# Experts' gate and up products with the weights still and 128 tokens streaming

## The chip, the cores and the metric

One Trainium2 chip, one of its cores. The metric is device time in microseconds (us) of one execution; the lower the better. The whole program is one launch.

## The reference, cut to what matters

The program runs two transformer blocks of two layers each over 256 tokens of width 1024, in float32. The change touches one part of it, the mixture of experts that closes the first block:

```
def swiglu(h, w_gate, w_up, w_down):
    return (jax.nn.silu(h @ w_gate) * (h @ w_up)) @ w_down

def moe_swiglu(h, w_router, w_gate, w_up, w_down):
    ...
    for e in range(N_EXPERTS):                       # 8 experts, top 2 of 8 are chosen for each token
        out = out + gates[..., e:e + 1] * swiglu(h, w_gate[e], w_up[e], w_down[e])
```

Here `h` is tokens x 1024, `w_gate[e]` and `w_up[e]` are 1024 x 2816, `w_down[e]` is 2816 x 1024.

## The kernel before, in words

Every weight is cut into units of 128 x 1024 numbers (512 KB). SyncE issues their loads into a ring of R = 11 slots (`raw`). ScalarE copies each unit to `whi` rounded to float32r (`split_high`, L436; a ring of H = 6 slots), and VectorE forms the remainder `low` (`split_low`, L440). A product of nearly full precision is then three float32r matmuls into the same PSUM: high x high (L445), high x low (L446), low x high (L447), by `product`. The activations are kept in the same two parts: `hTh` and `hTl` (hidden transposed), `aTh` and `aTl` (expert activation transposed).

The experts are one function, `swiglu`, on each engine, called inside a hardware loop over the 8 experts. Each expert gathers its (at most 128) tokens by a matmul with a one-hot matrix (`gather`, L1193), which also transposes them into `hTh`/`hTl`. It then takes STEPS = 11 steps of FW = 256 of the 2816 hidden columns. Step j has four "gu" units and two "down" units. A gu unit holds two 128-row slices of the input dimension, each with 256 gate and 256 up columns. Three things follow one another on TensorE in step j:

- the gate and up products of step j: for each of 8 slices of the input dimension, the tokens' slice (128 x 128) is the still operand and 512 weight columns stream (L1052); the result lies in one PSUM bank, tokens on partitions, with gate in columns 0 to 255 and up in 256 to 511;
- the transposes of the activation of step j - 1 (L1068), from `act` in SBUF into PSUM bank 6;
- the down products of step j - 2, with `aTh`/`aTl` still and 512 columns of `w_down` streaming.

ScalarE takes silu of the gate half (`gu_silu`, L1388) and VectorE multiplies it by the up half into `act` (L1858). After the transposes ScalarE copies bank 6 to `aTh` (L1392) and VectorE forms `aTl` (L1863). The next expert's gather and this expert's scatter of the previous result are woven between these through hooks. The order of the units is written out by `ffn_order`: down lags gu by two steps. Two PSUM banks, 4 and 5, take turns for gate and up (`gu_bank`).

The dense feed-forward stages elsewhere in the program (`dense`) already use the other form: a block of 128 weight columns is still and 256 tokens stream.

Of the kernel before, what the change touches and what calls it, by code (L numbers as in the profile page):

```python
# [24 lines left out]
P = 128  # L25
# [177 lines left out]
def build(nc, g, out, ctx):  # L203
# [171 lines left out]
    def high_slot(f, n):  # L375

        return (n + (N_MOE if f is fb else 0)) % H
# [65 lines left out]
    def product(pe, dst, ah, al, bh, bl, start, stop, **kw):  # L443

        pe.matmul(dst, ah, bh, start=start, stop=False, **kw)  # L445
        pe.matmul(dst, ah, bl, start=False, stop=False, **kw)  # L446
        return pe.matmul(dst, al, bh, start=False, stop=stop, **kw)  # L447
# [70 lines left out]
    def gu_bank(j, tiles):  # L518

        if tiles == T:  # L520
            return 0 if j == 0 else 4
        return 4 + j % 2
# [219 lines left out]
    def _(pe):  # L742
# [291 lines left out]
        def swiglu(f, n0, step0, tiles, it=0, first=(), hooks=None, gate=None):  # L1034

            units, steps = FFN_UNITS * it, STEPS * it
            for j in range(STEPS + 2):
                if j < STEPS:
                    if j == 0:
                        for sm, v in first:  # L1040
                            pe.wait_ge(sm, v)
                    elif j > 1 or tiles == 1:
                        pe.wait_ge(f.act, step0 + j + steps - (1 if tiles == 1 else 0))
                    for u in range(4):
                        n = n0 + POS["gu", j, u]
                        pe.wait_ge(f.lo, n + 1 + units)
                        for t in range(tiles):
                            for kk in range(2):
                                if j == 0 and t == 0 and hooks is None:
                                    pe.wait_ge(s_htl, first_ht + 2 * u + kk + 1)  # L1050
                                k = 2 * u + kk
                                last = product(pe, ps[:, gu_bank(j, tiles) + t, :],  # L1052
                                               hTh[:, k, t * P:(t + 1) * P], hTl[:, k, t * P:(t + 1) * P],
                                               whi[:, high_slot(f, n), kk * 512:(kk + 1) * 512],
                                               low[:, raw_slot(f, n), kk * 512:(kk + 1) * 512],
                                               start=k == 0, stop=k == DC - 1)
                        last.then_inc(f.used, 1)
                if hooks is not None and ("before_T", j) in hooks:
                    hooks["before_T", j]()
                if 1 <= j <= STEPS:  # L1060
                    i = j - 1
                    pe.wait_ge(f.act, step0 + i + 1 + steps)
                    if not (isinstance(it, int) and step0 + i == 0):
                        pe.wait_ge(f.atl, step0 + i + steps)
                    for t in range(tiles):
                        for kk in range(FK):
                            at = kk * S + t * P
                            last = pe.transpose(ps[:, 6, at:at + P], act[:, t, kk * P:(kk + 1) * P], ident)  # L1068
                    last.then_inc(f.tr, 1)
                if hooks is not None and ("after_T", j) in hooks:  # L1070
                    hooks["after_T", j]()
                if j == STEPS and gate is not None:
                    sum_gate(gate)
                if j >= 2:
                    i = j - 2

                    def unit(kk, t, half):
                        n = n0 + POS["down", i, kk]
                        return product(pe, ps[:, 2 * t + half, :],
                                       aTh[:, i % 2, kk, t * P:(t + 1) * P],  # L1080
                                       aTl[:, i % 2, kk, t * P:(t + 1) * P],
                                       whi[:, high_slot(f, n), half * 512:(half + 1) * 512],
                                       low[:, raw_slot(f, n), half * 512:(half + 1) * 512],
                                       start=i == 0 and kk == 0, stop=i == STEPS - 1 and kk == FK - 1)

                    pe.wait_ge(f.atl, step0 + i + 1 + steps)
                    for kk in range(FK):
                        pe.wait_ge(f.lo, n0 + POS["down", i, kk] + 1 + units)
                        if i < STEPS - 1 or tiles == 1:
                            for t in range(tiles):  # L1090
                                for half in range(2):
                                    last = unit(kk, t, half)
                            last.then_inc(f.used, 1)
                    if i == STEPS - 1 and tiles == T:
                        for t in range(T):
                            for half in range(2):
                                if (t, half) != (T - 1, 1):
                                    unit(0, t, half)
                                    unit(1, t, half).then_inc(s_part, 1)
                                else:  # L1100
                                    unit(0, t, half).then_inc(f.used, 1)
                                    unit(1, t, half).then_inc(f.used, 1)
            if gate in (1, 5):
                sum_cols(gate + 1)
# [182 lines left out]
    def _(ac):  # L1287
# [87 lines left out]
        def swiglu(f, n0, step0, tiles, it=0, skip=0, hooks=None, opening=None):  # L1375
            k = skip
            for j in range(STEPS + 2):
                while k < split_ahead(j):
                    if k == H and opening is not None:
                        opening()  # L1380
                    split_high(ac, f, n0 + k, it)
                    k += 1
                if j < STEPS:
                    ac.wait_ge(f.used, n0 + POS["gu", j, 3] + 1 + FFN_UNITS * it)
                    if not (isinstance(it, int) and step0 + j == 0):
                        ac.wait_ge(f.act, step0 + j + STEPS * it)
                    b = gu_bank(j, tiles)
                    ac.activation(gu_silu[:, 0:tiles, :], ps[:, b:b + tiles, 0:FW], ACT.Silu).then_inc(f.silu, 1)  # L1388
                if 1 <= j <= STEPS:
                    i = j - 1  # L1390
                    ac.wait_ge(f.tr, i + 1 + STEPS * it)
                    ac.activation(aTh[:, i % 2, :, 0:tiles * P],  # L1392
                                  ps[:, 6, :].rearrange("p (k s) -> p k s", k=FK)[:, :, 0:tiles * P], ACT.Copy)\
                        .then_inc(f.ath, 1)
                if hooks is not None and j in hooks:
                    hooks[j]()
# [265 lines left out]
    def _(ve):  # L1662
# [180 lines left out]
        def swiglu(f, n0, step0, tiles, it=0, skip=0, hooks=None, between=0, opening=None):  # L1843
            k = 0
            for j in range(STEPS + 2):
                while k < split_ahead(j):
                    if k == H and opening is not None:
                        opening()
                    if k >= skip:
                        split_low(ve, f, n0 + k, it)  # L1850
                    mods(spread(between, MOD_FFN_OVER, k - MOD_FFN_FROM))
                    k += 1
                if j < STEPS:
                    ve.wait_ge(f.silu, step0 + j + 1 + STEPS * it)
                    if not (isinstance(it, int) and j == 0):
                        ve.wait_ge(f.tr, j + STEPS * it)
                    b = gu_bank(j, tiles)
                    ve.tensor_tensor(act[:, 0:tiles, :], gu_silu[:, 0:tiles, :], ps[:, b:b + tiles, FW:2 * FW],  # L1858
                                     ALU.mult).then_inc(f.act, 1)
                if 1 <= j <= STEPS:  # L1860
                    i = j - 1
                    ve.wait_ge(f.ath, step0 + i + 1 + STEPS * it)
                    ve.tensor_tensor(aTl[:, i % 2, :, 0:tiles * P],  # L1863
                                     ps[:, 6, :].rearrange("p (k s) -> p k s", k=FK)[:, :, 0:tiles * P],
                                     aTh[:, i % 2, :, 0:tiles * P].bitcast(F32), ALU.subtract).then_inc(f.atl, 1)
                if hooks is not None and j in hooks:
                    hooks[j]()
# [554 lines left out]
```

## Time and profile before

| what | value |
|---|---|
| median of 2 runs | 1983.2 us (1980.59 and 1985.81) |
| span of the profiled execution | 1978.7 us |
| TensorE matmul busy | 1862.4 us, 94% of the span, 10670 instructions |
| TensorE weight load busy | 1603.6 us, 81% |
| VectorE busy | 1638.0 us, 83% |
| ScalarE busy | 1141.5 us, 58% |
| HBM read | 548.38 MB, 278 GB/s over the span |

The span runs from the first to the last instruction of the profiled execution; the page gives no other time for that execution, so the 4.5 us between the span and the median stand for what lies outside it. "Busy" on TensorE overlaps between neighbouring matmuls, since they are pipelined and their ends are modelled; how far apart two starts lie says more than how long one row is. TensorE's weight loads are rows of their own ("PEld") and run beside the matmul before. The experts take the stretch from about 500 to 1290 us.

### The profile page before, as it was taken

What the parts mean: (1) busy time and instruction counts of PE and PEld (TensorE: products, weight loads), DVE (VectorE), ACT (ScalarE), POOL (GpSimd) and SP (SyncE); (2) the same over time, 40 slices, a digit from 0 to 9 for tenths busy, and PEclk for the clock granted to TensorE, in tenths of its full rate; (3) what the DMA queues carried; (4) which work ended last, traced back from release to release, by engine and by line L of the source; (5) the groups of instructions that cost most, each with busy time, mean ns of one, the idle gap of its engine ahead of it and who ended that gap; (6) DMA issues with size and microseconds to landing.
All of it is one profiled execution on the core that took longest, in us unless ns stands there. A gap on an engine that the chain in (4) does not pass through costs nothing.

```text
span 1978.7 us, 32211 instructions
## 1 busy us (share of the span) xinstructions
PE 1862.4 (94%) x10670; PEld 1603.6 (81%) x10670; DVE 1638.0 (83%) x2193; ACT 1141.5 (58%) x1616; POOL 36.1 (2%) x47
## 2 busy tenths in 40 slices
PE   3999998988999999999999999988799998889998
PEld 2989998866788888888888888866689997679997
DVE  7999995768999999999999989887887758887554
ACT  3445444454777777777777777754654435545443
POOL 2000000000000000000000000000000000000000
PEclk9999999999999999999999999988999999999999
DMA  9978995557799999999999999958478874845772
GB/s 326 352 250 308 384 365 154 172 177 244 261 343 359 344 361 341 359 341 360 341 361 341 360 341 359 339 191 244 142 234 279 283 262 148 245 159 189 224 222 80
DMA packets 368485, 551.26 MB, mean 279 GB/s; under 512 B 35827, under 2 KB 293110, under 8 KB 368342
## 3 DMA queue, kind: packets, MB, share of 16 engines
q1 hardware_dynamic: 365392, 547.81, 82.3%
q10 hardware_dynamic: 2118, 1.46, 0.3%
q8 instruction: 65, 1.06, 0.2%
q14 instruction: 78, 0.64, 0.1%
q0 software_dynamic: 832, 0.30, 0.1%
HBM read 548.38 MB, written 1.08 MB: 278 GB/s over the span
## 4 chain that ended last, share of the span: by engine, by line
PE 84%; DVE 9%; ACT 3%; issue 2%; DMA 1%; POOL 0%; DVEq 0%; ACTq 0%; POOLq 0%
PE ps L445 25%; PE ps L447 25%; PE ps L446 25%; ACT prob L1410 2%; PE ps L960 2%; PE ps L1193 2%; DVE units_low L440 1%; DVE mod_acc L1733 1%; PE ps L1068 1%; PE ps L945 1%; DVE x_tokens L1760 1%; PE ps L796 1%; DVE x_normed L1759 1%; PE ps L771 1%; PE ps L933 1%
## 5 line engine op out<-in xcount | busy, mean ns | idle before, releaser
L440 DVE TENSOR_TENSOR units_low<-raw_units,units_high 128x1024 fp32r<-128x1024 f32 (+1 forms) x838 | 982.7, 1218 | 144.9 <-ACT units_high L436 142.1
L436 ACT ACTIVATE units_high<-raw_units 128x1024 fp32r<-128x1024 f32 (+1 forms) x838 | 846.3, 1057 | 300.0 <-PE ps L447 267.8
L445 PE MATMUL ps<-units_high,hT_high 128*128 128x512 f32 (+1 forms) x1040 | 412.1, 396 | 1.6 <-DVE hT_low L2161 1.4
L447 PE MATMUL ps<-units_high,hT_low 128*128 128x512 f32 (+1 forms) x1040 | 408.8, 393 | 0.0
L446 PE MATMUL ps<-units_low,hT_high 128*128 128x512 f32 (+1 forms) x1040 | 405.9, 390 | 0.0
L445 PE MATMUL ps<-hT_high,units_high 128*128 128x256 f32 x1248 | 346.3, 277 | 6.5 <-DVE hT_low L1802 5.2
L446 PE MATMUL ps<-hT_low,units_high 128*128 128x256 f32 x1248 | 345.5, 277 | 0.0
L447 PE MATMUL ps<-hT_high,units_low 128*128 128x256 f32 x1248 | 345.5, 277 | 0.0
L445 PE MATMUL ps<-units_high,aT_high 128*128 128x512 f32 x632 | 255.1, 404 | 1.2 <-DVE qkT L1997 0.6
L447 PE MATMUL ps<-units_high,aT_low 128*128 128x512 f32 x632 | 248.7, 393 | 0.0
L446 PE MATMUL ps<-units_low,aT_high 128*128 128x512 f32 x632 | 247.1, 391 | 0.0
L445 PEld LDWEIGHTS ps<-hT_high,units_high 128*128 128x128 f32 x1248 | 235.0, 188 | 8.7 <-issue 6.0
L446 PEld LDWEIGHTS ps<-hT_low,units_high 128*128 128x128 f32 x1248 | 235.2, 188 | 1.1
L447 PEld LDWEIGHTS ps<-hT_high,units_low 128*128 128x128 f32 x1248 | 235.0, 188 | 0.0
L445 PEld LDWEIGHTS ps<-units_high,hT_high 128*128 128x128 f32 x1040 | 197.0, 189 | 46.2 <-issue 3.3
L447 PEld LDWEIGHTS ps<-units_high,hT_low 128*128 128x128 f32 x1040 | 196.4, 189 | 43.1
L446 PEld LDWEIGHTS ps<-units_low,hT_high 128*128 128x128 f32 x1040 | 196.8, 189 | 42.3 <-issue 0.2
L1733 DVE SCALAR_TENSOR_TENSOR mod_acc<-mod_in,silu_c,mod_acc 128x1024 f32<-128x1024 f32 x168 | 213.9, 1280 | 9.5 <-DMA mod_in<-in_mod_w 3.7
L447 PEld LDWEIGHTS ps<-units_high,aT_low 128*128 128x128 f32 x632 | 118.7, 188 | 25.7
L445 PEld LDWEIGHTS ps<-units_high,aT_high 128*128 128x128 f32 x632 | 118.9, 188 | 24.4 <-issue 1.7
L446 PEld LDWEIGHTS ps<-units_low,aT_high 128*128 128x128 f32 x632 | 119.0, 188 | 23.7 <-issue 1.0
L1388 ACT ACTIVATE gu_silu<-ps 128x256 f32<-128x256 f32 x88 | 33.8, 384 | 145.0 <-PE ps L447 145.0
(283 smaller groups left out, 1430.2 us busy)
## 6 DMA issues: line engine op xcount, KB each, us to landing
raw_units<-in_moe_w_gate SPq DMA_DIRECT2D x352, 256.0 KB, 4.5
raw_units<-in_moe_w_up SPq DMA_DIRECT2D x352, 256.0 KB, 5.8
raw_units<-in_moe_w_down SPq DMA_DIRECT2D x176, 512.0 KB, 6.3
mod_in<-in_mod_w SPq DMA_DIRECT2D x96, 512.0 KB, 6.8
mod_in<-in_w_mod SPq DMA_DIRECT2D x96, 512.0 KB, 5.4
raw_units<-in_w_gu SPq DMA_DIRECT2D x176, 256.0 KB, 3.8
raw_units<-in_w_down SPq DMA_DIRECT2D x44, 512.0 KB, 4.2
raw_units<-in_w_in SPq DMA_DIRECT2D x32, 512.0 KB, 6.8
```

The lines of the kernel that those rows point to most:

```text
L436: eng.activation(whi[:rows, high_slot(f, n), 0:width], raw[:rows, raw_slot(f, n), 0:width], ACT.Copy).then_inc(f.hi, 1)
L440: eng.tensor_tensor(low[:rows, raw_slot(f, n), 0:width], raw[:rows, raw_slot(f, n), 0:width], whi[:rows, high_slot(f, n), 0:width].bitcast ...
L445: pe.matmul(dst, ah, bh, start=start, stop=False, **kw)
L446: pe.matmul(dst, ah, bl, start=False, stop=False, **kw)
L447: return pe.matmul(dst, al, bh, start=False, stop=stop, **kw)
L771: last = pe.matmul(ps[:, bank + half, :], ones, gate_acc(m)[:, half * 512:(half + 1) * 512], start=True, stop=True)
L796: last = pe.transpose(ps[:, 4 + b, at:at + P], xn[:, t, c * P:(c + 1) * P], ident)
L960: last = pe.matmul(dst, probT[:, j % 2, qt * key_tiles(second, 0) + kt, :], qkv[:, at - left * HD:at + (1 + right) * HD], start=kt == 0, s ...
L1193: last = pe.matmul(ps[:, 2 + c // 4, (c % 4) * P:(c % 4 + 1) * P], xn[:, t, c * P:(c + 1) * P], hot[:, t, :], start=t == 0, stop=t == T - 1)
L1388: ac.activation(gu_silu[:, 0:tiles, :], ps[:, b:b + tiles, 0:FW], ACT.Silu).then_inc(f.silu, 1)
L1410: last = ac.activation(prob[:, i % 2, qt, 0:nk], prob[:, i % 2, qt, 0:nk], ACT.Exp, bias=negm(qt, h), scale=-1.0, accum_out=sums(qt, h))
L1733: ve.scalar_tensor_tensor(out=acc, in0=mod_in[:, q % MOD_SLOTS, :], scalar=silu_c[:, at:at + 1], in1=acc, op0=ALU.mult, op1=ALU.add).then_ ...
```

## The change

In `swiglu`, gate and up are formed transposed. For each slice of the input dimension, four blocks of 128 weight columns (gate 0, gate 1, up 0, up 1) become the still operand one after the other and the 128 tokens of `hTh`/`hTl` stream. The result has hidden columns on partitions and tokens along the free dimension, four groups of 128 columns in the same PSUM bank, gate groups in the first half and up groups in the second. So `act` comes out transposed already: TensorE's transposes, their wait and their semaphore go, ScalarE copies `act` to `aTh` and VectorE subtracts from `act` instead of from PSUM, and `act` gets two buffers by turns. VectorE's write of `act` waits for the readers of two steps before (`f.ath`, `f.atl`) in place of `f.tr`; ScalarE's copy waits for `f.act` and for the last down unit that read the same half of `aTh`.

```
-                        for t in range(tiles):
-                            for kk in range(2):
...
-                                last = product(pe, ps[:, gu_bank(j, tiles) + t, :],
-                                               hTh[:, k, t * P:(t + 1) * P], hTl[:, k, t * P:(t + 1) * P],
-                                               whi[:, high_slot(f, n), kk * 512:(kk + 1) * 512],
-                                               low[:, raw_slot(f, n), kk * 512:(kk + 1) * 512],
-                                               start=k == 0, stop=k == DC - 1)
+                        for kk in range(2):
+                            k = 2 * u + kk
+                            for c in range(4):
+                                col = kk * 512 + c * P
+                                last = product(pe, ps[:, gu_bank(j, tiles), c * P:(c + 1) * P],
+                                               whi[:, high_slot(f, n), col:col + P],
+                                               low[:, raw_slot(f, n), col:col + P],
+                                               hTh[:, k, 0:P], hTl[:, k, 0:P], start=k == 0 and c == 0,
+                                               stop=k == DC - 1, skip_group_check=True)
...
-                if 1 <= j <= STEPS:
-                    i = j - 1
-                    pe.wait_ge(f.act, step0 + i + 1 + steps)
-                    if not (isinstance(it, int) and step0 + i == 0):
-                        pe.wait_ge(f.atl, step0 + i + steps)
-                    for t in range(tiles):
-                        for kk in range(FK):
-                            at = kk * S + t * P
-                            last = pe.transpose(ps[:, 6, at:at + P], act[:, t, kk * P:(kk + 1) * P], ident)
-                    last.then_inc(f.tr, 1)
...
-                    ac.wait_ge(f.tr, i + 1 + STEPS * it)
-                    ac.activation(aTh[:, i % 2, :, 0:tiles * P],
-                                  ps[:, 6, :].rearrange("p (k s) -> p k s", k=FK)[:, :, 0:tiles * P], ACT.Copy)\
+                    ac.wait_ge(f.act, step0 + i + 1 + STEPS * it)
+                    ac.wait_ge(f.used, n0 + FFN_UNITS * it + (POS["down", i - 2, FK - 1] + 1 if i >= 2 else 0))
+                    ac.activation(aTh[:, i % 2, :, 0:P], act[:, i % 2, :].rearrange("p (k s) -> p k s", k=FK), ACT.Copy)\
...
-                        ve.wait_ge(f.tr, j + STEPS * it)
+                        ve.wait_ge(f.ath, step0 + max(j - 1, 0) + STEPS * it)
+                        ve.wait_ge(f.atl, step0 + max(j - 1, 0) + STEPS * it)
...
-                    ve.tensor_tensor(act[:, 0:tiles, :], gu_silu[:, 0:tiles, :], ps[:, b:b + tiles, FW:2 * FW],
-                                     ALU.mult).then_inc(f.act, 1)
+                    ve.tensor_tensor(act[:, j % 2, :], gu_silu[:, 0, :], ps[:, b, FW:2 * FW], ALU.mult).then_inc(f.act, 1)
...
-                    ve.tensor_tensor(aTl[:, i % 2, :, 0:tiles * P],
-                                     ps[:, 6, :].rearrange("p (k s) -> p k s", k=FK)[:, :, 0:tiles * P],
+                    ve.tensor_tensor(aTl[:, i % 2, :, 0:P],
+                                     act[:, i % 2, :].rearrange("p (k s) -> p k s", k=FK),
                                      aTh[:, i % 2, :, 0:tiles * P].bitcast(F32), ALU.subtract).then_inc(f.atl, 1)
```

## Rows read from the trace of the kernel before

**Rows 1.** The page: busy time of each engine, and the span in 40 slices

```profile
PE 1862.4 (94%) x10670; PEld 1603.6 (81%) x10670; DVE 1638.0 (83%) x2193; ACT 1141.5 (58%) x1616; POOL 36.1 (2%) x47
...
PE   3999998988999999999999999988799998889998
...
PEclk9999999999999999999999999988999999999999
DMA  9978995557799999999999999958478874845772
```

**Rows 2.** Busy time by stretch: the middle of the experts' stage, and one expert

```profile
core 0: us, PE busy (x) PEld busy (x) DVE busy (x) ACT busy (x) POOL busy (x), PEclk, DMA share, GB/s
600.00:1200.00 600.00, 600.00 (x2791) 495.15 (x2790) 541.66 (x583) 446.05 (x553) 0.00 (x0) 1.00 1.03 351
592.70:691.59 98.89, 98.89 (x463) 81.62 (x462) 89.16 (x97) 73.57 (x91) 0.00 (x0) 1.00 1.03 351
```

**Rows 3.** Waits between 600 and 1200 us, all engines: in total, times, longest

```profile
ACT gu_silu L1388 <- PE ps L447: 109.6, 66, 1.8
ACT aT_high L1392 <- PE ps L1068: 24.8, 6, 4.1
...
DVE units_low L440 <- ACT units_high L436: 15.8, 42, 0.4
```

**Rows 4.** Groups between 500 and 1300 us: what the experts run on TensorE

```profile
L445 PE MATMUL ps<-units_high,hT_high 128*128 128x512 f32 x704 | 276.4, 393 | 1.4 <-DVE hT_low L2161 1.4
...
L445 PE MATMUL ps<-units_high,aT_high 128*128 128x512 f32 x352 | 144.4, 410 | 0.0
...
L1068 PE MATMUL ps<-table,act 128*128 128x128 f32 x176 | 33.5, 272 | 0.0
```

**Rows 5.** Order of time, TensorE, 512-column products: first and last of 48

```profile
799.62 0.39 PE L445 MATMUL ps<-units_high,hT_high 128*128 128x512 f32 x1
...
810.37 0.40 PE L447 MATMUL ps<-units_high,hT_low 128*128 128x512 f32 x1
```

**Rows 6.** Order of time, TensorE, around one step's transposes

```profile
589.33 0.40 PE L447 MATMUL ps<-units_high,hT_low 128*128 128x512 f32 x1
589.56 0.38 PE L1068 MATMUL ps<-table,act 128*128 128x128 f32 x2
589.70 0.48 PE L445 MATMUL ps<-units_high,aT_high 128*128 128x512 f32 x1
590.01 0.39 PE L446 MATMUL ps<-units_low,aT_high 128*128 128x512 f32 x1
```

**Rows 7.** The chain that ended last, around one gather and its successor

```profile
592.70 3.57 PE ps L1193 x32
...
691.59 3.57 PE ps L1193 x32
```

**Rows 8.** Order of time, TensorE, a dense stage: first and last of 34

```profile
282.05 0.28 PE L447 MATMUL ps<-hT_high,units_low 128*128 128x256 f32 x1
...
285.79 0.28 PE L447 MATMUL ps<-hT_high,units_low 128*128 128x256 f32 x1
```

**Rows 9.** Order of time, TensorE, products that stream 8 columns

```profile
495.31 0.39 PE L1182 MATMUL ps<-router_tmp,table 128*128 128x8 f32 x2 [0.20 <-DVE router_tmp L2138]
495.55 0.37 PE L1183 MATMUL ps<-router_tmp,table 128*128 128x8 f32 x2
...
496.22 0.37 PE L1186 MATMUL ps<-router_tmp,table 128*128 128x8 f32 x2
496.44 0.71 PE L778 MATMUL ps<-hT_high 128*128 128x512 f32 x2
```

**Rows 10.** Groups of weight loads: 128 columns, and 16 columns

```profile
L446 PEld LDWEIGHTS ps<-hT_low,units_high 128*128 128x128 f32 x1248 | 235.2, 188 | 1.1
...
L1157 PEld LDWEIGHTS ps<-hT_low,router_high_low 128*16 128x16 f32 x8 | 0.8, 95 | 0.1
```

**Rows 11.** Busy time in a stretch of attention

```profile
424.00:436.00 12.00, 9.12 (x73) 6.78 (x73) 11.46 (x28) 10.42 (x33) 0.00 (x0) 1.00 0.60 173
```

**Rows 12.** Order of time, TensorE, 512-column products where the clock was low

```profile
455.79 0.63 PE L446 MATMUL ps<-units_low,hT_high 128*128 128x512 f32 x1
456.22 0.63 PE L447 MATMUL ps<-units_high,hT_low 128*128 128x512 f32 x1
```

More of the change, by code:

```diff
@@ L1046, in swiglu @@
                         pe.wait_ge(f.lo, n + 1 + units)
-                        for t in range(tiles):
-                            for kk in range(2):
-                                if j == 0 and t == 0 and hooks is None:
-                                    pe.wait_ge(s_htl, first_ht + 2 * u + kk + 1)
-                                k = 2 * u + kk
-                                last = product(pe, ps[:, gu_bank(j, tiles) + t, :],
-                                               hTh[:, k, t * P:(t + 1) * P], hTl[:, k, t * P:(t + 1) * P],
-                                               whi[:, high_slot(f, n), kk * 512:(kk + 1) * 512],
-                                               low[:, raw_slot(f, n), kk * 512:(kk + 1) * 512],
-                                               start=k == 0, stop=k == DC - 1)
+                        for kk in range(2):
[7 more added lines that the diff above has]
+                                               stop=k == DC - 1, skip_group_check=True)
                         last.then_inc(f.used, 1)
```

## The prediction

> **What bounds the kernel now.** I began with the page's busy shares and its 40 slices [rows 1]. The reader is to see that TensorE is at 9 in every slice of the experts' stage (slices 11 to 25 or so), that DMA is at 9 there too, and that the granted clock is full. Two resources look full, so the next question is which one waits for the other. The table by stretch [rows 2] has TensorE busy for 600.00 of 600 us in the middle of the experts, VectorE for 541.66, ScalarE for 446.05. One expert takes 98.89 us, which is also the distance between two gathers in the chain that ended last [rows 7]. The waits settle it: between 600 and 1200 us every long wait is of an engine that waits for TensorE, or for another that does [rows 3]; none is of TensorE for anything, and nobody waits long for a DMA. So TensorE's own rate of products sets the end. The 351 GB/s is what that rate draws, not a limit that is felt: the loads run ahead through 11 slots and wait for `f.used`.
>
> So the change is a question of how many matmuls there are and how far apart they start. I take distances between starts, not the length of a row: rows of neighbouring matmuls overlap.
>
> **What is removed.** Gate and up of one step are 4 units x 2 slices x 3 products = 24 matmuls of 512 columns; of one expert 264 (the page's count, 704 for 8 experts in each of three forms, gives the same: 2112 / 8) [rows 4]. Forty-eight starts of this kind span 10.75 us, 47 distances: 0.2287 us each [rows 5]. That is 264 x 0.2287 = 60.4 us in each expert. The transposes start at 589.56; without them the first down product would start there and the second at 589.79; it starts at 590.01 [rows 6]. So a pair costs TensorE 0.22 us, 11 pairs 2.4 us in an expert. Together 62.8 us of the 98.9 us go. The check on the method: 396 products of 512 columns x 0.2287 = 90.6, the gather 3.57 [rows 7], 8 scatter products of the same width 1.8, transposes 2.4 + 0.2 for the pair on the one-hot matrix: 98.6 against 98.9 measured.
>
> **What is added.** The same columns of weights now need a still load each: 4 blocks x 8 slices x 3 products = 96 matmuls with 128 columns streaming in a step, 1056 in an expert. Each has a weight load of 128 columns. Before, one load served 512 streamed columns; now it serves 128. The question is the distance p between starts.
>
> - By the stream alone: 256 columns go by at 0.1133 us (3.74 us over 33 distances) [rows 8], 512 at 0.2287, so the stream costs 0.45 ns for a column and 128 columns would take 0.057 us.
> - By the load: products that stream only 8 columns, and so have almost no stream, still start 0.113 us apart (10 records from 495.31 to 496.44) [rows 9]. Nothing but the load of 128 columns is left to set this. The lengths of the loads say the same: 188 ns for 128 columns, 95 for 16 [rows 10]; 93 ns over 112 columns are 0.83 ns for a column, and 128 of them 106 ns, which is occupied once in each product, however well the constant part overlaps.
> - Load and stream together: the gather has 128-column loads and 128-column streams in the same stage, beside the same traffic: 32 records in 3.57 us, 0.1116 us each [rows 7]. As its operands are plain float32, each record may stream more slowly than float32r does; even so load and stream overlap wholly.
>
> So p is the greater of load and stream, not their sum. The lowest value I allow is 0.106 (the load without any constant), the highest 0.113 to 0.115 (8-column products, and some for the start of each unit). I take 0.112, next to the gather, the nearest row in shape and place. Then 1056 x 0.112 = 118.3 us in each expert.
>
> **Weighed against this.** The rows show no 128-column load at under 0.11 us a product. The Trainium skill, page TensorE: Matmul & The Clock Gate, section Back-to-back issue gap, gives about 81 ns for a product of 128 columns in a sustained stream of loads and matmuls. By that figure an estimate would be 1056 x 0.081 = 85.5 us, 22.7 us more in an expert and about 2165 us in all. The same page, Weight-path perf modes, excludes FP32 weights from its faster load, which suggests that the 81 ns are for narrower types; no run here shows those.
>
> **Edits I cost at nothing.** ScalarE's `aTh` copy and VectorE's `aTl` have the same 256 elements from SBUF in place of PSUM; both engines had 25 and 10 us idle in an expert [rows 2] and get more. If a read from SBUF costs more, the 55 us that are added to TensorE cover it. The new wait of VectorE for `f.ath`/`f.atl` of two steps before: behind it are `split_low`s of the next units, which TensorE needs; but the ScalarE copy it waits for stands behind no more than the silu of a step earlier, and lies a whole step, now about 14 us, back. ScalarE's new wait for `f.used` names the down unit of two steps before, which TensorE ended before it began the gate and up whose silu ScalarE has just done. TensorE's wait before the transposes goes; down products still wait for `f.atl`, which now comes earlier. None of these was late before [rows 3] and TensorE gets slower, so nothing else becomes late. TensorE issues two instructions (load and matmul) each 0.112 us, as the dense stage does at 0.1133 without stalls [rows 8], so instruction supply isn't new. SyncE's loads keep their order and only get later; with some 154 us for the same bytes DMA drops to about two thirds of its rate.
>
> **The sum.** In an expert +118.3 - 60.4 - 2.4 = +55.5 us; eight experts +444 us. On the span 1978.7 + 444 = 2423; the median lies 4.5 us above the span, so 2427 us. All of it is on the path, since TensorE has no gap in the stage to absorb any. With p = 0.106 it is +49.1 x 8 = +393, 2376 us; with 0.115 it is +58.6 x 8 = +469, 2452 us.
>
> **The rivals.**
>
> - Narrow float32r streams are slow. No row has a float32r matmul with under 256 columns. The nearest row on the dear side is the gather: a plain float32 product of 128 columns is two records, 0.223 us. If a narrow float32r product cost that, or the 0.2287 of the 512-column one, an expert would need 236 to 241 us for gate and up: +173 to +179, in all 3366 to 3412 us. For it: the kernel has no such width anywhere, so nothing excludes it. Against: 512, 480 and 256 columns show no step, 0.1133 is half of 0.2287. Chance 0.11, at about 3390.
> - Loads aren't hidden behind so short a stream: p = 0.106 + 0.057 = 0.163, +109.3 x 8 = +874, 2857 us. The gather speaks against it. Chance 0.03.
> - The other side: the load is no floor for these tiles, for instance because loads of float32r blocks overlap one another more than those of the float32 products that I read. Then the stream decides, p = 0.057, 60.2 us in place of 62.8: 2.6 us less in an expert, 1962 us, not slower than before. The place is gate and up alone, the price is 1056 x p, and the change breaks even at p = 62.8 / 1056 = 0.0595 us. For it: in the dense stage a load of 188 ns starts every 113 ns, so loads do overlap in part. Against it: the 8-column products, where a shorter distance had every chance to show. The page's 81 ns would lie between, on the slower side. Chance for p well under 0.106: 0.04.
> - The clock falls. TensorE would stream half as densely in two thirds of the stage. At the lower level of 1.2 GHz 512 columns start 0.43 us apart in place of 0.2287 [rows 12]; if the whole stage went so, 154.4 us for an expert become 309, and the program takes 3660 us. Against: attention, with 73 products and 9.12 us of 12 busy, kept the full 2.4 GHz [rows 11]. Chance 0.02.
>
> That the change doesn't do what it says isn't open: each product names a 128-column block, and the loads are counted above.
>
> **How the numbers follow.** The forecast, load-bound products at 0.106 to 0.115 us, has 0.80; the others 0.11, 0.03, 0.04 and 0.02. The predicted time is the forecast's, 2427 us. Its own bounds are 2376 and 2452; I go from 2385, as 0.106 leaves out a constant that every row shows, to 2465, for some loss at the 352 starts of units. That holds nearly all of the 0.80 and leaves the other cases out. Two per cent is about what a measurement of this kernel can tell from no change. Only the case with the stream as bound ends inside it, and a still better one beyond it: faster 0.01, same 0.03, slower 0.96.
>
> **What would show it.** Right: in the experts a group of 128x128 float32r products, 2816 in each of three forms, starting 0.112 us apart; L1068 gone; an expert at some 154 us; weight loads nearly as many microseconds as the stretch has; TensorE without waits and a granted clock of 1.00; DMA share at about 0.66; VectorE and ScalarE idle for longer, both behind TensorE. Wrong: a distance of 0.22 (slow narrow streams) or 0.163 (loads in series), a granted clock under 0.95, or a wait of TensorE for `aT_low` or `units_low` in the steps. The sum stands on p more than on all the rest: 0.001 us of it is 8.4 us of the program.

## The result, and the profile after

The changed kernel takes 2434.83 us (median of 2419.12 and 2450.54) against 1983.2 us before: 1.227 times as long, interval 1.222 to 1.231. The forecast was 2427 us. Four more executions, on another occasion, gave 2422.94 to 2443.99.

The page of the profiled execution (2450.54 us, span 2448.3 us), the lines that answer to [rows 1]:

```profile
PE 2331.8 (95%) x16830; PEld 2160.9 (88%) x16830; DVE 1655.7 (68%) x2193; ACT 1153.3 (47%) x1616; POOL 36.1 (1%) x47
...
PE   5999999899999999999999999999987999988998
...
PEclk9999999968999999999999999999999999999999
DMA  8969955726777767677677776777756788584673
```

The reader is to see four things: TensorE stays at 9 and has 6160 records more (8448 narrow products in, 2112 wide ones and 176 transposes out); DMA, at 9 in the experts before, is down to 6 and 7; VectorE and ScalarE did the same work in a longer time (VectorE's share falls from 83% to 68%); and the granted clock shows a 6 and an 8 in slices 9 and 10, where there was none before.

Busy time by stretch, answering to [rows 2], and the waits between 600 and 1600 us, answering to [rows 3]:

```profile
core 0: us, PE busy (x) PEld busy (x) DVE busy (x) ACT busy (x) POOL busy (x), PEclk, DMA share, GB/s
520.00:560.00 40.00, 40.00 (x186) 39.61 (x185) 11.99 (x12) 9.08 (x11) 0.00 (x0) 0.50 0.33 104
700.00:1300.00 600.00, 599.97 (x4797) 576.72 (x4797) 353.67 (x374) 290.52 (x355) 0.00 (x0) 1.00 0.72 226
```

```profile
ACT gu_silu L1377 <- PE ps L447: 310.9, 71, 4.7
DVE act L1848 <- ACT gu_silu L1377: 252.1, 71, 3.8
ACT units_high L436 <- PE ps L447: 180.3, 144, 1.6
```

In the second row of the first view TensorE and its weight loads are both busy nearly all the time; before, the loads were at 495 of 600. The rate fell from 351 to 226 GB/s, which is 0.64 of it, as forecast; the DMA share itself is 0.72, where 0.66 was expected. The first row is the odd one, and the one sign of being wrong that did appear in part (a granted clock under 0.95): TensorE is just as busy, at a granted clock of 0.50, which is 1.2 GHz. The waits say who sets the pace: everybody still waits for TensorE.

Order of time on TensorE, first and last of 28 gate and up products, answering to [rows 5]; and the same in the stretch of low clock, first and last of 12:

```profile
799.77 0.28 PE L447 MATMUL ps<-hT_high,units_low 128*128 128x128 f32 x1
...
802.79 0.27 PE L447 MATMUL ps<-hT_high,units_low 128*128 128x128 f32 x1
```

```profile
519.62 0.41 PE L446 MATMUL ps<-hT_low,units_high 128*128 128x128 f32 x1
...
521.97 0.41 PE L445 MATMUL ps<-hT_high,units_high 128*128 128x128 f32 x1
```

The distance between starts is 3.02 / 27 = 0.1119 us at full clock, and 2.35 / 11 = 0.2136 us at the low one. The chain that ended last, answering to [rows 7], gives one expert:

```profile
678.96 3.57 PE ps L1182 x32
...
832.84 3.57 PE ps L1182 x32
```

153.88 us for an expert, 98.89 before. It adds up: 1056 x 3.02 / 27 = 118.1, 132 down products x 0.2287 = 30.2, gather 3.57, scatter 1.8, the one-hot transposes 0.2: 153.9 us. TensorE has no gap here.

The low stretch begins in the first expert, 2.2 us after its first product, and lasts from 506.81 to 568.15 us, so 61.3 us:

```profile
504.63 0.33 PE L445 MATMUL ps<-hT_high,units_high 128*128 128x128 f32 x1 [1.41 <-DVE hT_low L2150]
...
506.70 0.32 PE L445 MATMUL ps<-hT_high,units_high 128*128 128x128 f32 x1
506.81 0.42 PE L446 MATMUL ps<-hT_low,units_high 128*128 128x128 f32 x1
...
543.73 0.73 PE L1195 MATMUL ps<-y_high,scatter_hot 128*128 128x512 f32 x1
...
565.91 0.73 PE L1195 MATMUL ps<-y_high,scatter_hot 128*128 128x512 f32 x1
...
568.15 0.43 PE L446 MATMUL ps<-units_low,aT_high 128*128 128x512 f32 x1
568.42 0.40 PE L447 MATMUL ps<-units_high,aT_low 128*128 128x512 f32 x1
```

Ahead of it TensorE had been idle for 1.41 us. Four scatter products of 512 columns at 543.73 did not bring the clock back; four more and the first down product, from 565.91 on, did.

### The profile page after: what moved, and what is told of

Read it like the earlier page. It is cut to its first block, busy times and chain, and to the rows that moved or that the text cites. A ratio compares the mean times of both kernels' runs of the same rounds, so it can differ in the third digit from the quotient of the medians.

```text
span 2448.3 us, 44475 instructions
## 1 busy us (share of the span) xinstructions
PE 2331.8 (95%) x16830; PEld 2160.9 (88%) x16830; DVE 1655.7 (68%) x2193; ACT 1153.3 (47%) x1616; POOL 36.1 (1%) x47
## 4 chain that ended last, share of the span: by engine, by line
PE 87%; DVE 7%; ACT 3%; issue 2%; DMA 1%; DVEq 0%; SPq 0%; ACTq 0%
PE ps L445 27%; PE ps L447 27%; PE ps L446 27%; PE ps L1182 1%; ACT prob L1399 1%; PE ps L960 1%; DVE units_low L440 1%; DVE mod_acc L1722 1%; PE ps L945 1%; DVE x_tokens L1749 1%; PE ps L796 1%; DVE x_normed L1748 1%; DMA mod_in<-in_w_mod 0%; PE ps L771 0%; PE ps L1195 0%
## 5 line engine op out<-in xcount | busy, mean ns | idle before, releaser
L445 PE MATMUL ps<-hT_high,units_high 128*128 128x128 f32 (+1 forms) x4064 | 1128.2, 278 | 8.2 <-DVE hT_low L1791 5.2
L446 PE MATMUL ps<-hT_low,units_high 128*128 128x128 f32 (+1 forms) x4064 | 1131.2, 278 | 0.0
L447 PE MATMUL ps<-hT_high,units_low 128*128 128x128 f32 (+1 forms) x4064 | 1131.1, 278 | 0.0
L445 PEld LDWEIGHTS ps<-hT_high,units_high 128*128 128x128 f32 x4064 | 787.8, 194 | 15.9 <-issue 7.8
L446 PEld LDWEIGHTS ps<-hT_low,units_high 128*128 128x128 f32 x4064 | 787.4, 194 | 4.4
L447 PEld LDWEIGHTS ps<-hT_high,units_low 128*128 128x128 f32 x4064 | 787.7, 194 | 0.0
L445 PE MATMUL ps<-units_high,hT_high 128*128 128x512 f32 (+1 forms) x336 | 135.9, 404 | 0.5 <-DVE hT_low L1791 0.4
L447 PE MATMUL ps<-units_high,hT_low 128*128 128x512 f32 (+1 forms) x336 | 132.6, 395 | 0.0
L446 PE MATMUL ps<-units_low,hT_high 128*128 128x512 f32 (+1 forms) x336 | 132.5, 394 | 0.0
L445 PEld LDWEIGHTS ps<-units_high,hT_high 128*128 128x128 f32 x336 | 64.9, 193 | 18.6 <-issue 3.5
```

## The experiments

Unless its section says otherwise, a kernel starts from the changed one. Edits are shown in `swiglu` on TensorE where nothing else is said.

### narrow_again: the changed kernel once more

> The changed kernel once more. Every theory of the distance between products (load, stream, issue) expects the time it had, about 2420 to 2450 us, and 0.112 us between starts of gate and up products. On the clock: if the low stretch of 61 us at the start of the first expert is a chance event that not each execution has, the times spread, between about 2415 us (no such stretch) and 2450 us (a full one); if it belongs to the kernel, each run shows a mean granted clock of 0.976 and about 2450 us.

Measured: 2422.94, 2424.28, 2437.28 and 2443.99 us, with mean granted clocks of 0.985, 0.985, 0.980 and 0.978. The profiled one (2424.28, span 2422.1 us) has no low stretch in the experts at all, though TensorE was idle for the same 1.41 us ahead of its first expert; its seven later experts take 154.05 us on average. The other three have no trace. An estimate of how long each spent at 0.50, span x (1 - clock) / 0.5, gives 73 us for the two quick ones, as for the kernel before (71), and 97 and 107 for the others (117 for the execution with the low stretch of 61 us). So a low stretch in the experts belongs to some executions and not to others; that it was there in the two slower ones, and shorter, is inferred from their mean clock. Not all of the spread need be its doing: the kernel before, measured beside them, went from 1980.39 to 1993.81. Without the low stretch the changed kernel takes some 2424 us.

### half_stream: half the tokens stream behind the same loads

```
-  last = product(pe, ps[:, gu_bank(j, tiles), c * P:(c + 1) * P], ..., hTh[:, k, 0:P], hTl[:, k, 0:P], ...)
+  last = product(pe, ps[:, gu_bank(j, tiles), c * P:c * P + 64], ..., hTh[:, k, 0:64], hTl[:, k, 0:64], ...)
```

> Gate and up of the experts stream 64 tokens in place of 128 (the products for the other 64 tokens are left out); the loads stay. Load theory (a load of 128 columns sets the distance): still 0.11 us between starts, the time as of the changed kernel within 10 us, about 2425. Stream theory (narrow float32r streams cost 0.87 ns for a column, which is also 0.112 us for 128): the distance falls towards 0.06, 8448 products x 0.05 = 420 us less, about 2000. Issue theory (TensorE's sequencer needs 0.056 us for each of the two instructions): unchanged, about 2425.

Measured: 3126.76 us (3124.51 and 3129.0), some 700 us above what any theory said. The trace shows why, and answers the question nevertheless. Order of time on TensorE, at the start of the second expert, one of the places where the clock fell; the first two rows are the first and last of 27 at full clock, the other two the first and last of 16 at the low one:

```profile
747.58 0.28 PE L447 MATMUL ps<-hT_high,units_low 128*128 128x64 f32 x1
...
750.49 0.28 PE L446 MATMUL ps<-hT_low,units_high 128*128 128x64 f32 x1
...
750.98 0.40 PE L446 MATMUL ps<-hT_low,units_high 128*128 128x64 f32 x1
...
754.18 0.40 PE L446 MATMUL ps<-hT_low,units_high 128*128 128x64 f32 x1
```

At full clock 64 columns take 2.91 / 26 = 0.1119 us, exactly what 128 take. Load theory (or issue theory) holds, stream theory falls. Then the clock falls in the middle of an uninterrupted row of products, and the distance is 3.20 / 15 = 0.213 us. Busy time by stretch, before and after the fall, and over the stage:

```profile
742.00:748.00 6.00, 6.00 (x31) 5.00 (x30) 4.81 (x5) 5.87 (x7) 0.00 (x0) 1.00 0.53 160
...
754.00:760.00 6.00, 6.00 (x30) 6.00 (x30) 1.22 (x1) 1.06 (x1) 0.00 (x0) 0.50 0.28 95
...
700.00:2400.00 1700.00, 1699.88 (x8662) 1625.34 (x8662) 648.28 (x674) 537.31 (x639) 0.00 (x0) 0.62 0.48 144
```

TensorE is busy throughout and is granted 0.62 on average. Ahead of this fall it had run 512-column down products at full clock without a gap; with half the stream behind each load the products did not keep it.

### half_load: half the load, the same stream

```
-  ps[:, gu_bank(j, tiles), c * P:(c + 1) * P], whi[..., col:col + P], low[..., col:col + P], ...
+  ps[0:64, gu_bank(j, tiles), c * P:(c + 1) * P], whi[..., col:col + 64], low[..., col:col + 64], ...
```

> Gate and up of the experts have 64 weight columns still in place of 128 (the products for the other 64 of each block are left out); the 128 tokens stream as before. Load theory: the load falls to about half, the distance to that of the stream or a little over, 0.057 to 0.065 us, so 8448 x 0.05 = 400 to 465 us less: 1960 to 2030. Stream theory: unchanged, 0.112 us, about 2425. Issue theory: unchanged, about 2425.

Measured: 2018.42 us (2015.82 and 2021.01), some 406 us under the changed kernel without its low stretch. First and last of 48 products on TensorE:

```profile
819.83 0.23 PE L445 MATMUL ps<-hT_high,units_high 128*64 128x128 f32 x1
...
822.65 0.22 PE L447 MATMUL ps<-hT_high,units_low 128*64 128x128 f32 x1
```

2.82 / 47 = 0.0600 us. The same count of instructions starts at nearly half the distance, so neither the issue nor the stream of 128 columns set 0.112 us; the load of 128 weight columns did. The whole gains 406 us and not the full 8448 x 0.052 = 439. TensorE now waits for units, which is 15 us of the missing 33; the rest was not followed up. Waits between 600 and 1300 us:

```profile
PE ps L445 <- DVE units_low L440: 15.1, 6, 2.9
...
ACT units_high L436 <- DMA raw_units<-in_moe_w_up: 9.2, 20, 1.6
```

Behind such a wait the clock fell here too, but it came back without one wide product:

```profile
706.12 0.27 PE L445 MATMUL ps<-hT_high,units_high 128*64 128x128 f32 x1 [1.92 <-DVE units_low L440]
...
706.73 0.31 PE L447 MATMUL ps<-hT_high,units_low 128*64 128x128 f32 x1
...
709.71 0.31 PE L445 MATMUL ps<-hT_high,units_high 128*64 128x128 f32 x1
...
710.07 0.22 PE L446 MATMUL ps<-hT_low,units_high 128*64 128x128 f32 x1
```

The second and third rows are the first and last of 29 products at the low level, 2.98 / 28 = 0.106 us apart. From about 706.5 to 709.9 us, so 3.4 us, the clock is low, then the distance is 0.060 again. The changed kernel streams the same 128 columns at each product, but behind twice the load, and stayed low for 61 us.

### double_stream: 256 columns behind the same loads

```
-  ps[:, gu_bank(j, tiles), c * P:(c + 1) * P], ..., hTh[:, k, 0:P], hTl[:, k, 0:P], ...
+  ps[:, gu_bank(j, tiles), (c % 2) * S:(c % 2 + 1) * S], ..., hTh[:, k, 0:S], hTl[:, k, 0:S], ...
```

> Gate and up of the experts stream 256 columns in place of 128 behind the same loads (the other 128 columns are old activations, and the four blocks share two halves of the bank, so the sums aren't gate and up). Load theory: the stream now just fills the load's time, 0.1133 us as in the dense stages, 8448 x 0.0015 = 12 us more, about 2437. Stream theory (0.87 ns for a column, or a slow mode under 256 columns that ends here): 0.22 us, +900 us, or 0.1133. Issue theory: as load theory.

Measured: 2444.46 us (2444.24 and 2444.69). First and last of 31 products:

```profile
821.56 0.28 PE L447 MATMUL ps<-hT_high,units_low 128*128 128x256 f32 x1
...
824.97 0.28 PE L447 MATMUL ps<-hT_high,units_low 128*128 128x256 f32 x1
```

3.41 / 30 = 0.1137 us, in place of 0.1119. Twice the stream costs 20 us in all, where 12 were expected; 8448 x 0.0018 = 15 of them lie in the distance, the rest was not followed up. The profiled execution has no low stretch in the experts, and both runs agree within half a microsecond.

### old_no_transposes: one part of the change alone

The kernel before, with the change's lines for `act`, `aTh` and `aTl` on ScalarE and VectorE, and on TensorE:

```
-                if 1 <= j <= STEPS:
-                    i = j - 1
-                    pe.wait_ge(f.act, step0 + i + 1 + steps)
...
-                            last = pe.transpose(ps[:, 6, at:at + P], act[:, t, kk * P:(kk + 1) * P], ident)
-                    last.then_inc(f.tr, 1)
```

> The kernel before with one part of the change alone: gate and up keep the tokens still and 512 weight columns streaming, but the transposes and their wait are left out, and act goes straight from SBUF to aTh and aTl (so the down products get untransposed activations). If TensorE's own work is the bound, 88 x 0.22 us = 19 us go, about 1963, ratio 0.990. If the transposes' time would be filled by another wait (for a unit's low part, or a DMA at 351 GB/s), nothing goes: 1982.

Measured: ratio 0.9938, interval 0.9915 to 0.9961, so about 12 us gained (8 to 17), between the two expectations. The trace tells how each was right for a part of the experts. The chain that ended last, gathers of the first experts, and the waits between 600 and 1200 us:

```profile
591.05 3.57 PE ps L1183 x32
687.50 3.57 PE ps L1183 x32
783.98 3.57 PE ps L1183 x32
881.53 3.57 PE ps L1183 x32
```

```profile
ACT units_high L436 <- DMA raw_units<-in_moe_w_up: 61.2, 149, 1.2
DVE units_low L440 <- ACT units_high L436: 33.4, 110, 0.9
ACT units_high L436 <- DMA raw_units<-in_moe_w_down: 29.3, 83, 0.9
...
PEld ps L445 <- DVE units_low L440: 6.2, 20, 0.6
```

The first two experts take 96.45 and 96.48 us, 2.4 less than 98.89: that is the transposes' price as predicted. The next takes 97.55 and the later ones some 97.3. ScalarE now waits for DMA 232 times, which it hardly did before: 66 units of 0.524 MB in 97.3 us are 356 GB/s. Once the lead of the 11 slots is spent, the loads set the pace, and 1.6 of the 2.4 us stay. So the 351 GB/s of the kernel before was not its limit, but stood within 2% of one.

### gap_narrow, gap_old_form, gap_narrow_wide: can the narrow products lift the clock?

In gap_narrow (the changed kernel) and gap_old_form (the kernel before) ScalarE keeps TensorE waiting ahead of the first expert:

```
         for half in range(2):
+            if half == 1:
+                for _ in range(6):
+                    link(ac.activation(yh[:, :], xn[:, 0, :], ACT.Copy))
             ac.wait_ge(s_gat, half + 1)
```

gap_narrow_wide is gap_narrow with, on TensorE, after the first waits of expert 0:

```
+                            pe.wait_ge(f.lo, n0 + 1)
+                            slot = high_slot(f, n0)
+                            for _ in range(24):
+                                pe.matmul(ps[:, 6, :], whi[:, slot, 0:P], whi[:, slot, 0:512], start=True, stop=True)
```

> The changed kernel with an idle time of TensorE put in just before the first expert's gate and up: ScalarE makes six idle copies of 128x1024, each 1.0 us, ahead of the second half of the gathered tokens (6 us or so by themselves). Trap theory (with only 128 columns streamed behind each load of 128, TensorE is too little used to be given back its full clock once it has lost it; only the 512-column scatter and down products, which first come after two steps, do that): each execution now has the low stretch of 40 to 65 us, mean clock about 0.976, 2424 + 6 + 24 = 2454 or some more, with little spread. Chance theory (the long low stretch comes and goes whatever the work is): the spread of the changed kernel stays, 2430 to 2450, with no link to the gap.

> The kernel before with the same idle time. Trap theory: here 512 columns stream behind each load, so the clock may fall in the gap but is back within a few us of work: 1982 + 6 + 2 to 4 = 1990 to 1993. Chance theory or a long recovery whatever the work: 1982 + 6 + 20 to 30 = 2010 to 2018, with a low stretch of some 60 us.

> The changed kernel with the idle time, and then 24 idle products that stream 512 columns before the first narrow one (5.5 us at full clock, some 9 if they begin at the low one). Trap theory: they bring the clock back, and the narrow products keep it: no low stretch beyond a few us, 2424 + 6 + 5 to 9 = 2435 to 2440, less than with the gap alone although there is more work. Chance theory: as the gap alone plus 5 to 9, about 2460.

Measured: gap_narrow 2454.14 us (2446.86 to 2461.93), with a mean clock of 0.972 to 0.976 in all four executions. gap_old_form 1995.1 us, ratio 1.0036 (1.0016 to 1.0056): 3 to 11 us more than the kernel before, whose median was 1987.05 on this occasion. gap_narrow_wide 2438.68 us (2432.54 to 2446.84), clock 0.983 to 0.986: it does 24 products more than gap_narrow and is 15 us faster. Busy time by stretch of 20 us, gap_narrow first, then gap_old_form, then gap_narrow_wide; the last three numbers of a row are granted clock, DMA share and GB/s:

```profile
500.00:520.00 20.00, 13.17 (x77) 12.98 (x75) 11.58 (x21) 12.04 (x13) 0.00 (x0) 0.64 0.09 27
520.00:540.00 20.00, 20.00 (x95) 20.00 (x95) 5.23 (x5) 4.39 (x5) 0.00 (x0) 0.50 0.32 105
540.00:560.00 20.00, 20.00 (x120) 19.61 (x120) 6.98 (x8) 5.84 (x7) 0.00 (x0) 0.66 0.34 107
```

```profile
500.00:520.00 20.00, 12.78 (x66) 10.69 (x66) 12.74 (x29) 15.91 (x19) 0.00 (x0) 0.83 0.11 35
520.00:540.00 20.00, 20.00 (x91) 16.37 (x90) 20.00 (x22) 14.69 (x19) 0.00 (x0) 1.00 0.97 322
```

```profile
500.00:520.00 20.00, 13.17 (x82) 11.65 (x80) 9.90 (x20) 11.09 (x13) 0.00 (x0) 0.83 0.00 1
520.00:540.00 20.00, 20.00 (x178) 19.83 (x176) 9.24 (x10) 7.81 (x11) 0.00 (x0) 1.00 0.65 194
```

After the same idle time, 512-column products are back at full clock by 520 us. The narrow ones run at 0.50, busy without a break, through the next 20 us and into the third stretch; the clock is back at 553.4 us, right behind the first four scatter products (551.11 to 552.9). Wide products ahead of the narrow ones bring the clock back, and the narrow ones then keep it. Chance theory falls. All three times fit the trap theory, gap_old_form by its 8 us over the kernel before where the theory gave 8 to 11 (its 1995.1 itself is 2 us above the expected 1993). One thing does not fit it as worded: in the changed kernel's own trace the same four scatter products, at 543.73, did not bring the clock back. So some wide products are not always enough, and how many it takes was not measured; 24 were.

### bridged, wide_start: the changed kernel without the trap

bridged puts six such 512-column products ahead of the first wait, where TensorE idles 1.4 us after the first gather; wide_start puts 24 behind that wait. Neither has the gap of the three kernels above.

```
+                        if isinstance(it, int) and hooks is not None:
+                            pe.wait_ge(f.lo, n0 + 1)
+                            slot = high_slot(f, n0)
+                            for _ in range(6):
+                                pe.matmul(ps[:, 6, :], whi[:, slot, 0:P], whi[:, slot, 0:512], start=True, stop=True)
                         for sm, v in first:
                             pe.wait_ge(sm, v)
```

> The changed kernel with six idle products that stream 512 columns behind the first gather, while TensorE waits 1.4 us for the first expert's tokens, so at no cost of their own. Trap theory: TensorE comes to the narrow products without an idle time before them, and the clock is lost less often: mean granted clock 0.983 to 0.986 in all executions, 2420 to 2428, with no run at 2435 to 2450 as the changed kernel alone has them. If the narrow products lose the clock by themselves at the start of an expert, the spread of the changed kernel stays.

> The changed kernel with 24 idle products of 512 columns between the first wait and the first narrow product (5.5 us). Trap theory: no low stretch in the first expert in any execution, 2424 + 5.5 = 2430, mean clock 0.983 to 0.986, highest run under 2440. Otherwise the changed kernel's spread, 2428 to 2455.

Measured: bridged 2423.91 us (six executions, 2420.14 to 2430.66; clocks 0.984 to 0.987), at its highest 3 us above the expected 2428. wide_start 2432.47 us (five, 2426.17 to 2433.08; clocks 0.983 to 0.987). Neither profiled execution has a low stretch in the experts. Of the changed kernel's six executions three were at 2437 or above, with clocks of 0.980 or less; of these eleven none was. If it were chance, such a split would come once in 34 times (20 / 680). It is not a clean comparison either: the changed kernel did not run beside these two, and the kernel before spread less on this occasion (1979.96 to 1988.98). So that the wide products removed the low stretch is likely here, and not shown. bridged has the lowest median of all forms of the change, and is still 1.2215 times the kernel before (1.2190 to 1.2241), an interval that overlaps that of the changed kernel.

## Why the prediction was right

**The bound.** TensorE had no gap before and has none now; the added time of an expert is the added time of its products. The waits of both kernels confirm it, and so does an expert that adds up to 153.9 us from TensorE's records alone.

**The distance p.** Predicted 0.112, measured 0.1119 us. The reason given, that the load of 128 weight columns sets it and load and stream overlap wholly, was put to the test by changing each by itself: stream 64, 128 and 256 columns and p is 0.1119, 0.1119 and 0.1137; load 64 columns and it is 0.0600, where the stream alone would give 0.057. So p is the greater of the two, to within 0.003 us. Instruction issue, which the prediction dismissed without a row that could tell it from the load, is excluded by the same 0.0600. The rows that bore the forecast were the right ones, the 8-column products and the gather [rows 7, 9].

**The removed terms.** 60.4 us of wide products go, as a fact of the count. The transposes' 2.4 us an expert were confirmed by old_no_transposes in its first two experts. What the prediction didn't see is that in the old form only two thirds of it could be had for long, because DMA came next. In the new form DMA has room, and the expert adds up to 153.9 us without transposes, so the term stands there.

**The sum.** +55.5 us an expert predicted, +55.0 measured, +440 for eight. Span 2423 predicted; 2422.1 in the profiled execution of narrow_again, which has no low stretch. The 4.5 us added for what lies outside the span were too many: wherever a run has both figures they differ by some 2.2 us, and the rest of the 4.5 lies between executions. The median of 2434.83 lies 8 us above the forecast, because one of its two executions had the low stretch.

**The clock.** This is the step that was sized wrongly. The rival was priced as all or nothing, 3660 us with chance 0.02, on the ground that attention kept the full clock [rows 11]. That row was no measure: none of its products is a narrow float32r one. Nor was it the only such row. In another stretch of the kernel before with attention's products, where TensorE also idled more, the clock wasn't full:

```profile
1700.00:1720.00 20.00, 14.08 (x98) 10.97 (x95) 14.48 (x42) 15.48 (x38) 0.74 (x2) 0.91 0.86 263
```

What happened is in between. In the profiled execution the clock fell at the start of the first expert and stayed low for 61.3 us, which cost some 26 us; two more of the six executions were 13 and 20 us over the quick ones, with mean clocks that fit a shorter low stretch. The price was small, so the number held, but nothing in the prediction bounded it: that part was luck. With half the stream, as in half_stream, it was 700 us. Why the fall comes in one execution and not in the next, behind the same 1.41 us of idle time, stays open. With a longer idle time ahead the mean clock was 0.976 or less in all four executions; with wide products ahead of the first narrow one it was 0.983 or more in all fifteen.

**The other rivals.** Slow narrow float32r streams (3366 to 3412 us) are excluded by 0.1119 at both 64 and 128 columns, and loads in series with the stream (0.163) likewise. The rival on the other side needed p under 0.0595: no kernel with 128-column loads had it, and half_load shows that it takes half the load to come near. The page TensorE: Matmul & The Clock Gate of the Trainium skill, Back-to-back issue gap, has 81 ns for a product of 128 columns; for float32r this case's runs give 112 to 114 ns at three widths of stream, and the measurement decides.

**Edits at nothing.** ScalarE's copy to `aTh` from SBUF takes 409 ns where it took 379 from PSUM, which is hidden. The only wait before this copy is 0.6 us in all, for TensorE; TensorE itself waited 0.4 us in the 1000 between 600 and 1600.

## What to carry to other kernels

Which operand is held still is a question of how many columns stream behind each load: where a load of 128 float32r columns takes 0.112 us, anything under 256 streamed columns is paid for at that price, and swapping the operands of a product with 128 tokens turns one load per 512 columns into one per 128. Count loads, and look for the shortest products already in the trace: they show the floor. Before an operation is taken off a full engine, ask what is next; here DMA at 351 GB/s stood right behind a TensorE without gaps, so that only two thirds of the transposes' time could be won.

## What the hardware showed that I had not expected

A TensorE that is busy without a break can still be kept at 1.2 GHz. With loads of 128 and streams of 128 columns it kept the full clock through seven experts, with the wide down products between, but did not get it back soon once it was lost: 40.00 of 40 us busy at 0.50. With 64 streamed columns it lost it again and again, mean 0.62 over 1700 us. With loads of 64 and streams of 128 columns it was back after 3.4 us. With 256 or 512 columns streamed no low stretch in the experts of a profiled execution was longer than 7 us.

The Trainium skill's page TensorE: Matmul & The Clock Gate, section Why this matters for your kernels, advises to keep TensorE continuously busy. These rows show that busy time alone isn't enough. 24 wide products ahead of the narrow ones brought the clock back in gap_narrow_wide, and saved 15 us net; four did in gap_narrow, and four did not in the changed kernel.
